# Twenty dots of gathered rows move from VectorE to TensorE and ScalarE; picks and first gathers stand earlier

## The chip, the cores and the metric

The kernel runs on one core of one Trainium2 chip. The metric is the time of one execution on the device in microseconds (us); the kernel before takes 3178.87 us (median of three runs).

## The reference

Two transformer blocks in float32 on 256 tokens of width 2048. Only the end of the second one matters here, a feed-forward of 16384 experts of which each token takes 128:

```python
q = einsum("bsd,dhk->bshk", h, w_pq)                 # queries of 8 heads
sub = einsum("bshpk,hpnk->bshpn", q, peer_keys)      # scores of 2 x 128 keys a head
s, i = top_k(sub, 16)                                # best keys of each side
cand = s[0][:, None] + s[1][None, :]                 # their 256 pairs
top_s, pos = top_k(cand, 16); idx = cidx[pos]        # 16 experts of a head
gate = softmax(top_s)
u = take(peer_u, idx)                                # (128 tokens, 8 x 16, 2048)
a = gelu(einsum("td,thkd->thk", x_blk, u)) * gate    # one dot of 2048 for each
v = take(peer_v, idx)
out = x + einsum("thk,thkd->td", a, v)               # then a norm
```

The tokens are two halves of 128; a half has 8 heads x 16 picks, so there are 2 x 128 = 256 "rows": row n is one expert's row of u for each of the 128 tokens of half n // 128 (one token on each partition), 1 MB.

## The kernel before

Everything up to the key scores is a chain of matmul stages. `out_and_queries_stage` is the last of these: it multiplies w_out and w_peer_q, 8 tiles of 4 slabs, each slab split by ScalarE (L194) and VectorE (L199) into a high and a low part. In its last slabs VectorE already picks the experts of the first four units (a unit is one head of one half): `best_keys`, `best_pairs` and `experts_of_pairs` in turn, which end in `index`, the numbers that a gather needs. Its GpSimd part issues the first 8 gathers once the stage's last matmul is done.

`peer_stage` follows. There:

- GpSimd gathers rows of u (`gather_row`, L1918) into a ring of GR = 8 buffers, `rows`; the gather of row n + 8 waits until row n was read (`freed`), and the first of each 16 also until its unit was picked (`p.picked`).
- VectorE makes one dot for each row (L2308: multiply with h2 and sum, 2048 elements on each partition), in the order of n, into column n of `weight`. Between the dots stand the 36 parts that pick the experts of the other 12 units, spread over the first PICK_DOTS = 232 rows, and a few small steps: `shift` and `share` (the softmax's), `weigh`, `index_pieces`.
- TensorE and ScalarE do nothing until `weigh(0)`, at row 130; then they spread the weights of the first half into `by_expert` (L2384, L2416 to L2432).
- After the last dot VectorE weighs the second half, helps to spread it (L2280, L2285) and adds pieces of v: `add_piece` (L2331) takes gathered half rows of v (L2249). Ahead of the first piece it waits for `summed`, which SyncE loads from x (L2223).
- SyncE loads the first six slabs of v (512 KB each) and then `summed` (1 MB) as soon as the dots 248 to 252 are done; it waits on `freed`.
- TensorE multiplies slabs of v with `by_expert` (L2391) to the end.

The order within an engine is the order in which the program writes it; between engines only semaphores order.

Of the kernel before, what the change touches and what calls it, by code (L numbers as in the profile page):

```python
# [23 lines left out]
ALU = mybir.AluOpType  # L24
AX = mybir.AxisListType

P = 128
# [3 lines left out]
DC = D // P  # L31
# [13 lines left out]
PH, NKEYS, TOPK = 8, 128, 16  # L45
PICKS = PH * TOPK
RING = 4
KPE_W = 256
GR = 8
# [1862 lines left out]
PICK_DOTS = 232  # L1912
# [10 lines left out]
def out_and_queries_stage(core, block, w_out, w_queries, gain_rows, keys_in_dram, x_home, peer_u, p):  # L1923
# [9 lines left out]
    nc, base, outs = core.nc, core.tiles, core.outs  # L1933
# [10 lines left out]
    with ExitStack() as local:  # L1944
# [5 lines left out]
        p.x_kept = x_kept  # L1950
# [147 lines left out]
        @block.gpsimd  # L2098
        def _(pool):
            pool.wait_ge(core.slabs_used, (base + 8) * RING + 2)  # L2100
            pool.wait_ge(p.picked, 1)
            for n in range(GR):
                gather_row(nc, p, n, peer_u)
# [54 lines left out]
def peer_stage(core, block, p, peer_u, peer_v, counts, gain, out):  # L2158
# [14 lines left out]
    nc = core.nc  # L2173
# [4 lines left out]
    with ExitStack() as local:  # L2178
# [3 lines left out]
         pieces_indexed, slab_used) = core.new(  # L2182
# [3 lines left out]
            "stored", "final_steps", "pieces_used", "pieces_indexed", "expert_slabs_used")  # L2186
# [4 lines left out]
        place = core.place  # L2191
        by_expert = place("by_expert", [P, NH, NKEYS, P], at=-48 * KB)
# [19 lines left out]
        def half_of(half):  # L2212
            return slice(half * PICKS, (half + 1) * PICKS)

# [22 lines left out]
        @block.gpsimd  # L2237
        def _(pool):
            for n in range(GR, UNITS * TOPK):
                if n % TOPK == 0:  # L2240
                    pool.wait_ge(p.picked, n // TOPK + 1)
                pool.wait_ge(freed, n + 1)
                gather_row(nc, p, n, peer_u)
            pool.wait_ge(freed, NH * PICKS + GR)
            pool.wait_ge(pieces_indexed, NH)
            for n in range(UNITS * TOPK):
                if n >= GR:
                    pool.wait_ge(piece_used, n - GR + 1)
                nc.gpsimd.indirect_dma_start(  # L2249
                    pieces[:, n % GR, :], None, v_pieces,  # L2250
                    bass.IndirectOffsetOnAxis(ap=piece_at[n % NH][:, n // NH:n // NH + 1], axis=0)
                ).then_inc(piece_landed[n % GR], 16)

        @block.vector
        def _(dve):
# [45 lines left out]
            parts_left = 3 * (UNITS - EARLY_UNITS)  # L2301
            for u in range(UNITS):
                for j in range(TOPK):
                    n = u * TOPK + j
                    dve.wait_ge(landed[n % GR], n // GR * 16 + 16)
                    if n:
                        dve.wait_ge(freed, n + GR - 1)
                    nc.vector.tensor_tensor_reduce(out=junk[:, n % 2, :], in0=rows[:, n % GR, :], in1=p.h2[:, u // PH, :],  # L2308
                                                   scale=1.0, scalar=0.0, op0=ALU.mult, op1=ALU.add,
                                                   accum_out=weight[:, n:n + 1]).then_inc(freed, 1)  # L2310
                    k = n * parts_left // PICK_DOTS
                    if k < (n + 1) * parts_left // PICK_DOTS and k < parts_left:
                        PICK_PARTS[k % 3](core, dve, step, EARLY_UNITS + k // 3, p.sub, p)
                    if n in (4 * TOPK + 6, PICK_DOTS + 1):
                        shift(u // PH)
                    if n in (5 * TOPK + 6, 15 * TOPK + 6):
                        share(u // PH)
                    if j == 2 and u == PH:
                        weigh(0)
                    if n == PICK_DOTS + 4:  # L2320
                        index_pieces()
# [43 lines left out]
        def _(pe):  # L2365
# [29 lines left out]

            turn(0)
# [12 lines left out]
        def _(act):  # L2409
# [43 lines left out]
            exponentiate(0)  # L2453
# [218 lines left out]
```

## Time and profile before

| | |
|---|---|
| median of three runs | 3178.87 us (3177.93 to 3179.3) |
| the profiled execution's own time | 3179.94 us |
| its span, first to last instruction | 3177.8 us |
| VectorE busy over the span | 2180.5 us (69%) |
| TensorE busy | 2404.4 us (76%) |
| ScalarE busy | 1109.8 us (35%) |
| row 0's dot starts | 1942.45 us |
| row 150's dot starts | 2347.15 us |
| row 255's dot starts, the last | 2619.75 us |
| the first piece of v is added | 2631.05 us |
| TensorE and ScalarE spread the first half's weights | 2301 to 2466 us |

The span's times count from the first instruction. Busy shares are means over stages that have different limits; the stretch of the dots, from 1942 to 2622 us, has to be read by itself.

### The profile page before, as it was taken

Reading aid. Unit: us, or ns where it says so; the run is one execution under the profiler, and the core shown is the slowest. Engines: PE = TensorE matmul, PEld = TensorE weight load, DVE = VectorE, ACT = ScalarE, POOL = GpSimd, SP = SyncE. Lnnn points to the kernel's source line nnn. Section 1 sums busy time; section 2 is a strip of 40 time slices with the busy share of each in tenths; the row PEclk is TensorE's granted clock in tenths of the full one; section 3 lists DMA queues with packets and bytes.
Section 4 is the critical chain, followed back from the end, with each engine's and each line's share of the span. In section 5 each row is a group of like instructions: output and inputs, shape, how many; then the busy total and the mean of one; then the engine's idle time right before and its main releaser. Section 6 shows DMA issues by size and latency. Waiting matters only on the chain. (4 is left out here: it accounts for less than half of the span.)

```text
span 3177.8 us, 29960 instructions
## 1 busy us (share of the span) xinstructions
PE 2404.4 (76%) x10393; PEld 1830.5 (58%) x10393; DVE 2180.5 (69%) x2958; ACT 1109.8 (35%) x1876; POOL 826.6 (26%) x571
## 2 busy tenths in 40 slices
PE   6899999999999999999999993000033006999993
PEld 5667778888888878888777893000033005444441
DVE  3997565544454565555546568999999998565668
ACT  4345554344434444535554441000099005000000
POOL 0300001010100000000000004767667664544445
PEclk9999999999999999999999997555555559999997
DMA  8443455665656546546435666999999995999998
GB/s 224 150 148 113 167 173 189 195 186 194 189 185 186 197 159 218 185 147 205 140 113 167 210 205 253 419 389 387 392 396 389 396 398 188 405 410 409 409 409 342
DMA packets 294486, 813.25 MB, mean 256 GB/s; under 512 B 33113, under 2 KB 73281, under 8 KB 260320
## 3 DMA queue, kind: packets, MB, share of 16 engines
q1 hardware_dynamic: 220400, 408.87, 38.8%
q0 software_dynamic: 73728, 402.69, 31.9%
q8 instruction: 67, 1.10, 0.1%
q14 instruction: 51, 0.42, 0.0%
q10 hardware_dynamic: 240, 0.18, 0.0%
HBM read 807.48 MB, written 4.19 MB: 255 GB/s over the span
## 5 line engine op out<-in xcount | busy, mean ns | idle before, releaser
L199 DVE TENSOR_TENSOR wl<-ring,wh 128x1024 fp32r<-128x1024 f32 (+2 forms) x616 | 732.7, 1231 | 646.0 <-ACT wh L194 643.4
L194 ACT CAST wh<-ring 128x1024 fp32r<-128x1024 f32 (+2 forms) x616 | 609.4, 1039 | 672.7 <-PE ps L215 620.5
L213 PE MATMUL ps<-wh,th 128*128 128x512 f32 (+1 forms) x1632 | 646.3, 396 | 27.8 <-DVE wl L199 23.0
L1918 POOL DMA_INDIRECT expert_rows<-in_peer_u,index x256 | 481.9, 1882 | 626.8 <-PE ps L2004 437.9
L214 PE MATMUL ps<-wl,th 128*128 128x512 f32 (+1 forms) x1632 | 637.2, 390 | 0.0
L215 PE MATMUL ps<-wh,tl 128*128 128x512 f32 (+1 forms) x1632 | 636.9, 390 | 0.0
L2308 DVE CUSTOM_DVE_ANT_0 junk<-expert_rows,h 128x2048 f32<-128x2048 f32 x256 | 570.1, 2286 | 6.2 <-DMA expert_rows<-in_peer_u,index 5.3
L2331 DVE SCALAR_TENSOR_TENSOR x_and_pieces<-expert_pieces,const,x_and_pieces 128x1024 f32<-128x1024 f32 x256 | 327.7, 1283 | 170.5 <-DMA expert_pieces<-in_peer_v,piece_index 83.4
L2391 PE MATMUL ps<-expert_slabs,by_expert 128*128 128x512 f32 x1024 | 439.7, 592 | 0.7 <-ACT by_expert L2432 0.7
L213 PEld LDWEIGHTS ps<-wh,th 128*128 128x128 f32 x1632 | 309.8, 190 | 98.9 <-issue 18.7
L215 PEld LDWEIGHTS ps<-wh,tl 128*128 128x128 f32 x1632 | 309.6, 190 | 64.7
L214 PEld LDWEIGHTS ps<-wl,th 128*128 128x128 f32 x1632 | 310.1, 190 | 61.1
L2391 PEld LDWEIGHTS ps<-expert_slabs,by_expert 128*128 128x128 f32 x1024 | 194.5, 190 | 245.3 <-issue 244.4
L2373 PE MATMUL ps<-const,keys_of 128*128 128x128 f32 x4 | 1.4, 448 | 316.2 <-DVE index L1903 316.2
L803 POOL TENSOR_TENSOR square<-relu 128x512 f32<-128x512 f32 x32 | 48.4, 1536 | 661.3 <-ACT relu L758 661.3
L2384 PE MATMUL ps<-col_hot,row_hot 128*128 128x128 f32 x512 | 105.9, 374 | 128.7 <-ACT row_hot L2427 102.0
L213 PE MATMUL ps<-wh,fh 128*128 128x512 f32 x512 | 199.5, 390 | 0.0
L215 PE MATMUL ps<-wh,fl 128*128 128x512 f32 x512 | 199.2, 389 | 0.0
L214 PE MATMUL ps<-wl,fh 128*128 128x512 f32 x512 | 199.2, 389 | 0.0
L2373 PEld LDWEIGHTS ps<-const,keys_of 128*128 128x128 f32 x4 | 0.6, 204 | 316.7 <-DVE index L1903 316.7
L2384 PEld LDWEIGHTS ps<-col_hot,row_hot 128*128 128x128 f32 x512 | 92.2, 267 | 142.5 <-ACT col_hot L2421 57.8
L2249 POOL DMA_INDIRECT expert_pieces<-in_peer_v,piece_index x128 | 133.5, 1043 | 138.3 <-DVE x_and_pieces L2331 124.4
(329 smaller groups left out, 2668.9 us busy)
## 6 DMA issues: line engine op xcount, KB each, us to landing
ring<-in_w_in SPq DMA_DIRECT2D x80, 1024.0 KB, 5.2
ring<-in_w_up SPq DMA_DIRECT2D x64, 1024.0 KB, 5.5
ring<-in_w_down SPq DMA_DIRECT2D x64, 1024.0 KB, 5.1
expert_slabs<-in_peer_v SPq DMA_DIRECT2D x128, 512.0 KB, 6.8
ring<-in_w_in SPq DMA_DIRECT2D x68, 512.0 KB, 4.8
ring<-in_w_out SPq DMA_DIRECT2D x32, 1024.0 KB, 5.0
ring<-in_w_peer_q SPq DMA_DIRECT2D x16, 1024.0 KB, 5.2
ring<-in_w_ukv SPq DMA_DIRECT2D x8, 1024.0 KB, 5.5
```

The lines of the kernel that those rows point to most:

```text
L194: self.nc.scalar.copy(self.wh[:, i % 2, two, 0:w], self.ring[:, i, two, 0:w]).then_inc(self.high_ready, 1)
L199: self.nc.vector.tensor_tensor(self.wl[:, i % 2, two, 0:w], self.ring[:, i, two, 0:w], self.wh[:, i % 2, two, 0:w].bitcast(F32), ALU.subtr ...
L213: mm(o, hi, wh, start=start and k == 0, stop=False)
L214: mm(o, hi, wl, start=False, stop=False)
L215: last = mm(o, lo, wh, start=False, stop=stop and k == 3)
L803: nc.gpsimd.tensor_tensor(square[:, n % 2, half, :], r, r, ALU.mult).then_inc(squared, 1)
L1918: nc.gpsimd.indirect_dma_start(p.rows[:, n % GR, :], None, peer_u, bass.IndirectOffsetOnAxis(ap=p.index[:, n:n + 1], axis=0)).then_inc(p.l ...
L2249: nc.gpsimd.indirect_dma_start(pieces[:, n % GR, :], None, v_pieces, bass.IndirectOffsetOnAxis(ap=piece_at[n % NH][:, n // NH:n // NH + 1] ...
L2308: nc.vector.tensor_tensor_reduce(out=junk[:, n % 2, :], in0=rows[:, n % GR, :], in1=p.h2[:, u // PH, :], scale=1.0, scalar=0.0, op0=ALU.mu ...
L2331: nc.vector.scalar_tensor_tensor(out=summed[:, half, :], in0=pieces[:, n % GR, :], scalar=weight[:, c:c + 1], in1=summed[:, half, :], op0= ...
L2384: mm(core.ps[:, 4 + i // 4, i % 4 * P:(i % 4 + 1) * P], row_hot[:, i, :], col_hot[:, i, :], start=True, stop=True).then_inc(hot_used, 1)
L2391: end = mm(core.ps[:, 2 * half + q, :], by_expert[:, half, m, :], slabs[:, m % SLOTS, q * 512:(q + 1) * 512], start=m == 0, stop=m == NKEY ...
```

## The change

Twenty of the rows of the first half, n = 4, 10, ..., 118, are no longer read by VectorE. TensorE turns the row's 16 blocks of 128 x 128 (`turn_row`, into PSUM banks 0 to 3), ScalarE copies each bank to SBUF (`lay_row`, four copies of 512), and TensorE multiplies the 16 blocks with the 16 blocks of h2, turned once at the start in the same way, into one 128 x 128 product, whose diagonal holds the 128 dots. VectorE reads that diagonal seven rows later (`diagonal`: multiply with the identity and sum, 128 elements). A buffer that held such a row is free for the next gather when TensorE has turned it. The pick parts are spread over the first 150 rows in place of 232; `shift(1)` and `index_pieces` keep their places. The first eight gathers no longer wait for the stage's last matmul but each for the last reader of what its buffer lies on. ScalarE's `exponentiate(0)` follows its copies of row 70, and TensorE's `turn(0)` follows row 118.

```diff
-PICK_DOTS = 232
+PICK_DOTS = 150
+LATE_DOT = 232
+PE_ROWS = tuple(range(4, 120, 6))
+PE_LAG = 7
...
+        p.x_kept, p.h2_ready = x_kept, h2_ready
...
         @block.gpsimd
         def _(pool):
-            pool.wait_ge(core.slabs_used, (base + 8) * RING + 2)
             pool.wait_ge(p.picked, 1)
             for n in range(GR):
+                if n < RING:
+                    pool.wait_ge(core.low_ready, (base + 7) * (2 * RING) + (2 * n + 2))
+                else:
+                    pool.wait_ge(core.slabs_used, (base + 7) * RING + (RING + 1 + n % 2))
                 gather_row(nc, p, n, peer_u)
...
+        h2_turned = place("h2_turned", [P, DC, P], at=0)
+        row_turned = place("row_turned", [P, DC, P], at=8 * KB)
...
+        by_order = []
+        for n in range(UNITS * TOPK):
+            by_order += [n] * (n not in PE_ROWS) + [n - PE_LAG] * (n - PE_LAG in PE_ROWS)
+
+        def row_read(n):
+            if n in PE_ROWS:
+                return quarters_turned, 4 * (PE_ROWS.index(n) + 2)
+            return freed, GR + by_order.index(n) + 1
...
-                pool.wait_ge(freed, n + 1)
+                pool.wait_ge(*row_read(n - GR))
                 gather_row(nc, p, n, peer_u)
...
+            def dot(n):
+                dve.wait_ge(landed[n % GR], n // GR * 16 + 16)
+                k = by_order.index(n)
+                if k:
+                    dve.wait_ge(freed, k + GR - 1)
+                nc.vector.tensor_tensor_reduce(out=junk[:, k % 2, :], in0=rows[:, n % GR, :], in1=p.h2[:, n // PICKS, :],
+                                               scale=1.0, scalar=0.0, op0=ALU.mult, op1=ALU.add,
+                                               accum_out=weight[:, n:n + 1]).then_inc(freed, 1)
+
+            def diagonal(n):
+                i, k = PE_ROWS.index(n), by_order.index(n)
+                dve.wait_ge(rows_dotted, i + 1)
+                dve.wait_ge(freed, k + GR - 1)
+                nc.vector.tensor_tensor_reduce(out=junk[:, k % 2, 0:P], in0=core.ps[:, (7, 5)[i % 2], 0:P],
+                                               in1=core.ident, scale=1.0, scalar=0.0, op0=ALU.mult, op1=ALU.add,
+                                               accum_out=weight[:, n:n + 1]).then_inc(freed, 1)
+
             for u in range(UNITS):
                 for j in range(TOPK):
                     n = u * TOPK + j
-                    dve.wait_ge(landed[n % GR], n // GR * 16 + 16)
-                    if n:
-                        dve.wait_ge(freed, n + GR - 1)
-                    nc.vector.tensor_tensor_reduce(out=junk[:, n % 2, :], in0=rows[:, n % GR, :], in1=p.h2[:, u // PH, :],
-                                                   scale=1.0, scalar=0.0, op0=ALU.mult, op1=ALU.add,
-                                                   accum_out=weight[:, n:n + 1]).then_inc(freed, 1)
+                    if n not in PE_ROWS:
+                        dot(n)
+                    if n - PE_LAG in PE_ROWS:
+                        diagonal(n - PE_LAG)
                     k = n * parts_left // PICK_DOTS
                     if k < (n + 1) * parts_left // PICK_DOTS and k < parts_left:
                         PICK_PARTS[k % 3](core, dve, step, EARLY_UNITS + k // 3, p.sub, p)
-                    if n in (4 * TOPK + 6, PICK_DOTS + 1):
+                    if n in (4 * TOPK + 6, LATE_DOT + 1):
                         shift(u // PH)
                     if n in (5 * TOPK + 6, 15 * TOPK + 6):
                         share(u // PH)
                     if j == 2 and u == PH:
                         weigh(0)
-                    if n == PICK_DOTS + 4:
+                    if n == LATE_DOT + 4:
...
+            def turn_row(src, banks_read):
+                if banks_read:
+                    pe.wait_ge(quarters_laid, banks_read)
+                for c in range(DC):
+                    last = nc.tensor.transpose(core.ps[:, c // 4, c % 4 * P:(c % 4 + 1) * P], src[:, c * P:(c + 1) * P], core.ident)
+                    if c % 4 == 3:
+                        last.then_inc(quarters_turned, 1)
+
+            def dot_by_tensor(i, n):
+                pe.wait_ge(landed[n % GR], n // GR * 16 + 16)
+                turn_row(rows[:, n % GR, :], 4 * i + 4)
+                if i >= 2:
+                    pe.wait_ge(freed, GR + by_order.index(PE_ROWS[i - 2]) + 1)
+                for c in range(DC):
+                    if c % 4 == 0:
+                        pe.wait_ge(quarters_laid, 4 * (i + 1) + c // 4 + 1)
+                    last = mm(core.ps[:, (7, 5)[i % 2], 0:P], row_turned[:, c, :], h2_turned[:, c, :],
+                              start=c == 0, stop=c == DC - 1)
+                last.then_inc(rows_dotted, 1)
+
+            pe.wait_ge(core.outs_free, (core.outs - 1) * 2 + 6)
+            pe.wait_ge(p.scores_out, 2 * 4)
+            pe.wait_ge(p.h2_ready, 1)
+            turn_row(p.h2[:, 0, :], 0)
+            for i, n in enumerate(PE_ROWS):
+                dot_by_tensor(i, n)
             turn(0)
...
-            exponentiate(0)
+            def lay_row(dst, i):
+                for q in range(4):
+                    act.wait_ge(quarters_turned, 4 * i + q + 1)
+                    if i >= 2 and q == 0:
+                        act.wait_ge(rows_dotted, i - 1)
+                    nc.scalar.copy(dst[:, 4 * q:4 * q + 4, :], core.ps[:, q, :].rearrange("p (c t) -> p c t", c=4)).then_inc(
+                        quarters_laid, 1)
+
+            lay_row(h2_turned, 0)
+            for i, n in enumerate(PE_ROWS):
+                lay_row(row_turned, i + 1)
+                if n == 4 * TOPK + 6:
+                    exponentiate(0)
```

Three places where the instructions stand otherwise. GpSimd, the first gathers; what stands in brackets is what each waits for (the name after `waits` in the second stage's rows is only that of a semaphore number used before for something else: it is `freed` or, in its one row here, `row_quarters_turned`). Before:

```order
L2098 UNCONDITIONAL_BRANCH [waits barrier_Pool_Activation_PE_DVE_SP_gather]
L1918 DMA expert_rows<-in_peer_u,index 128x2048 [waits unit_picked_16,slabs_used]
L1918 DMA expert_rows<-in_peer_u,index 128x2048 x7
L2237 UNCONDITIONAL_BRANCH
L1918 DMA expert_rows<-in_peer_u,index 128x2048 [waits taps_in_1] x8
```

And now:

```order
L1921 DMA expert_rows<-in_peer_u,index 128x2048 [waits low_ready,unit_picked_16]
L1921 DMA expert_rows<-in_peer_u,index 128x2048 [waits low_ready] x3
L1921 DMA expert_rows<-in_peer_u,index 128x2048 [waits slabs_used] x4
L2255 UNCONDITIONAL_BRANCH
L1921 DMA expert_rows<-in_peer_u,index 128x2048 [waits taps_in_1] x4
L1921 DMA expert_rows<-in_peer_u,index 128x2048 [waits normed_4]
L1921 DMA expert_rows<-in_peer_u,index 128x2048 [waits taps_in_1] x3
```

The eight first gathers have waits of their own, and gather 12 waits for row 4's turning. VectorE, the dots ahead of the third pick part (`experts_of_pairs`, L1895); `ISA junk` is a dot (or, from `ps`, a diagonal), and each is followed by a short `ISA const` that stores its sum. Before:

```order
L2308 ISA junk,const<-expert_rows,h_12674 128x2048
L2308 ISA const 128x1
L2308 ISA junk,const<-expert_rows,h_12674 128x2048
L2308 ISA const 128x1
L1895 TENSOR_TENSOR one_hot<-const,place_f 128x256 x2
```

And now:

```order
L2326 ISA junk,const<-expert_rows,h_12674 128x2048
L2326 ISA const 128x1
L2334 ISA junk,const<-ps,const 128x128
L2334 ISA const 128x1
L2326 ISA junk,const<-expert_rows,h_12674 128x2048
L2326 ISA const 128x1
L2326 ISA junk,const<-expert_rows,h_12674 128x2048
L2326 ISA const 128x1
L1895 TENSOR_TENSOR one_hot<-const,place_f 128x256 x2
```

A diagonal has come in, and a pick part follows every fourth or fifth row in place of every sixth or seventh. TensorE, between the key scores and `turn(0)`. Before:

```order
L2016 MATMUL ps<-keys_turned,peer_queries_turned 128x128 x8
L2364 UNCONDITIONAL_BRANCH
L2373 MATMUL ps<-const,keys_of 128x128 x2
L2376 MATMUL ps<-const 128x128
L2397 UNCONDITIONAL_BRANCH
```

And now, with 19 more pairs like the last two ahead of the transposes of `keys_of`:

```order
L2019 MATMUL ps<-keys_turned,peer_queries_turned 128x128 x8
L2398 UNCONDITIONAL_BRANCH
L2434 MATMUL ps<-const,h_12674 128x128 x16
L2434 MATMUL ps<-const,expert_rows 128x128 x16
L2446 MATMUL ps<-h_turned,row_turned 128x128 x16
```

TensorE's queue now holds 16 transposes and 16 matmuls for each of the 20 rows, in front of everything else that it does in this stage.

## Rows read from the trace of the kernel before

**Rows 1.** Windows: PE, PEld, DVE, ACT, POOL busy us, TensorE's clock, DMA share, GB/s.

```profile
2030.00:2050.00 20.00, 0.00 (x0) 0.00 (x0) 19.66 (x35) 0.00 (x0) 14.13 (x8) 0.50 1.01 420
...
2250.00:2270.00 20.00, 0.00 (x0) 0.00 (x0) 19.86 (x23) 0.00 (x0) 14.96 (x9) 0.50 0.97 378
...
2310.00:2330.00 20.00, 8.29 (x32) 7.12 (x32) 19.86 (x33) 19.71 (x58) 11.75 (x7) 0.50 0.99 395
...
2590.00:2610.00 20.00, 0.00 (x0) 0.00 (x0) 19.90 (x22) 0.00 (x0) 15.22 (x8) 0.50 1.01 419
```

**Rows 2.** Waits of VectorE and of GpSimd, 1900 to 2600 (us, times, longest).

```profile
DVE junk L2308 <- DMA expert_rows<-in_peer_u,index: 5.3, 7, 2.5
...
POOL expert_rows L1918 <- DVE const L2308: 120.8, 36, 4.1
```

**Rows 3.** Timeline of ScalarE, GpSimd and VectorE where the dots begin (start, us, engine).

```profile
1938.73 1.52 ACT L2073 ACTIVATE key_scores<-ps,small 128x512 f32<-128x512 f32 x2 [1.31 <-PE ps L2016]
...
1926.04 2.36 DVE L199 TENSOR_TENSOR wl<-ring,wh 128x1024 fp32r<-128x1024 f32 x2 [2.35 <-ACT wh L194]
...
1936.61 1.15 POOL L1918 DMA_INDIRECT expert_rows<-in_peer_u,index  x1 [437.93 <-PE ps L2004]
...
1942.45 2.29 DVE L2308 CUSTOM_DVE_ANT_0 junk<-expert_rows,h 128x2048 f32<-128x2048 f32 x1 [2.54 <-DMA expert_rows<-in_peer_u,index]
```

**Rows 4.** Timeline of VectorE, dots on either side of the three pick parts.

```profile
2060.76 2.29 DVE L2308 CUSTOM_DVE_ANT_0 junk<-expert_rows,h 128x2048 f32<-128x2048 f32 x1
...
2062.97 2.29 DVE L2308 CUSTOM_DVE_ANT_0 junk<-expert_rows,h 128x2048 f32<-128x2048 f32 x1
...
2068.37 2.29 DVE L2308 CUSTOM_DVE_ANT_0 junk<-expert_rows,h 128x2048 f32<-128x2048 f32 x1
...
2079.44 2.28 DVE L2308 CUSTOM_DVE_ANT_0 junk<-expert_rows,h 128x2048 f32<-128x2048 f32 x1
...
2084.60 2.29 DVE L2308 CUSTOM_DVE_ANT_0 junk<-expert_rows,h 128x2048 f32<-128x2048 f32 x1
...
2563.97 0.76 DVE L1895 TENSOR_TENSOR one_hot<-const,place_f 128x256 f32<-128x256 f32 x2
...
2566.66 2.29 DVE L2308 CUSTOM_DVE_ANT_0 junk<-expert_rows,h 128x2048 f32<-128x2048 f32 x1
```

**Rows 5.** Timeline of VectorE: the dots of rows 150, 247 and 255, and small operations.

```profile
2347.15 2.29 DVE L2308 CUSTOM_DVE_ANT_0 junk<-expert_rows,h 128x2048 f32<-128x2048 f32 x1
...
2602.04 2.29 DVE L2308 CUSTOM_DVE_ANT_0 junk<-expert_rows,h 128x2048 f32<-128x2048 f32 x1
...
2619.75 2.28 DVE L2308 CUSTOM_DVE_ANT_0 junk<-expert_rows,h 128x2048 f32<-128x2048 f32 x1
2621.96 0.08 DVE L2308 DVE_READ_ACCUMULATOR2_ANT const<- 128x1 f32 x1
...
2625.27 1.10 DVE L2280 TENSOR_SCALAR row_hot<-const,turned_keys,turned_weight 128x128 f32<-128x128 f32 x4
2631.05 1.28 DVE L2331 SCALAR_TENSOR_TENSOR x_and_pieces<-expert_pieces,const,x_and_pieces 128x1024 f32<-128x1024 f32 x1 [4.68 <-DMA x_and_pieces<-out]
```

**Rows 6.** TensorE: 16 transposes, four matmuls (8 records), lengths of all such records.

```profile
1854.20 1.91 PE L1991 MATMUL ps<-const,keys 128*128 128x128 f32 x16
...
2316.62 2.08 PE L2384 MATMUL ps<-col_hot,row_hot 128*128 128x128 f32 x8 [3.09 <-ACT row_hot L2427]
...
L2384 PE MATMUL ps<-col_hot,row_hot x512: 275/421/583, 2301.5 to 2689.3; 128*128 128x128 f32 x171
```

**Rows 7.** L1918 from 2070 to 2560: from issue to landing.

```profile
DMA to landing us min/median/max: 7.1/9.4/11.3
```

**Rows 8.** Row 255's gather in GpSimd's timeline, and L1918 from 2585 to 2606.

```profile
2605.45 1.91 POOL L1918 DMA_INDIRECT expert_rows<-in_peer_u,index  x1 [0.30 <-issue]
...
DMA to landing us min/median/max: 9.3/10.5/14.2
```

**Rows 9.** The first pieces of v (L2249) from 2600 to 2640: from issue to landing.

```profile
DMA to landing us min/median/max: 5.9/8.3/8.6
```

More of the change, by code:

```diff
@@ L1949, in out_and_queries_stage @@
             "factor_steps", "keys_turned", "keys_copied", "scored", "scores_out", "h2_ready", "pick_steps")
-        p.x_kept = x_kept
+        p.x_kept, p.h2_ready = x_kept, h2_ready
         p.picked, = core.new("unit_picked")
@@ L2181, in peer_stage @@
          iota_in, sums_in, x_back, gain_in, added, sums, mean_ready, rooted, normed, stored, final, piece_used,
-         pieces_indexed, slab_used) = core.new(
+         pieces_indexed, slab_used, quarters_turned, quarters_laid, rows_dotted) = core.new(
             "dve_done", "rows_used", "shifted", "exponentiated", "gelued", "weighted", "picks_turned",
@@ L2185, in peer_stage @@
             "sums_in", "x_back", "gain_in", "x_added", "x_sums", "mean_ready", "rooted", "normed",
-            "stored", "final_steps", "pieces_used", "pieces_indexed", "expert_slabs_used")
+            "stored", "final_steps", "pieces_used", "pieces_indexed", "expert_slabs_used",
+            "row_quarters_turned", "row_quarters_laid", "rows_dotted")
         cols_hot = core.new("cols_hot_low", "cols_hot_high")
```

## The prediction

> **What bounds the kernel now.** I read the windows first. Through the dots VectorE is busy 19.7 to 19.9 us of every 20, and TensorE does nothing or little [rows 1]. But the DMA share is 0.97 to 1.01 as well, so that view alone names two candidates. The bytes part them: about 420 GB/s while the ring of eight buffers fills (2030), 378 in the middle (2250), and 419 again near the end (2590), where VectorE has no picks left [rows 1]. In the middle the DMA moves less than it can. The waits say why: VectorE waited for a gathered row 5.3 us in all, in seven waits, the longest of them on row 0; GpSimd waited 120.8 us for VectorE to read a buffer [rows 2]. So the dots and the picks, one after the other on VectorE, bound this stretch. The DMA is the limit close behind: 1.049 MB at 420 GB/s is 2.50 us a row. A dot takes 2.21 us (2060.76 to 2062.97), and the three pick parts of a unit add 5.40 - 2.21 = 3.19, 5.16 - 2.21 = 2.95 and 2.69, together 8.83 us [rows 4]. Spread over 232 rows the 12 units (106 us) add 0.46 to each row: 2.67 us, above 2.50. That is the order of things which the change disturbs: a row without picks costs VectorE 2.21, less than the DMA's 2.50.
>
> **The start.** VectorE's first dot waits 2.54 us for row 0, whose gather was issued at 1936.61, after the stage's last matmul [rows 3]. Now gathers 0 to 3 follow VectorE's last four splits (the last ends at 1928.4 [rows 3]); one takes under 6 us to land here (1936.61 to 1942.45), so those rows are there when VectorE is ready. It then waits for ScalarE's scores, which end at 1938.73 + 1.52 = 1940.25 [rows 3]. First dot at 1940.3, 2.1 us earlier. The small waits on rows 1 to 6 go too.
>
> **The first 150 rows.** VectorE has 130 dots there x 2.213 = 287.7 us and all 36 pick parts = 106.0. `shift`, `share` and `weigh` stand in this stretch as before, about 1.5. The 20 diagonals are not in this trace. Below, four operations on 128 elements take 1.10 [rows 5], with the 0.08 of the accumulator's read 0.36 or less each; a dot of 2048 takes 2.21, of which at most 2.13 scales with its length by the same 0.08. I take 0.30 each, between 0.20 and 0.50: 6.0 us. Row 150 would be reached at 1940.3 + 287.7 + 106.0 + 1.5 + 6.0 = 2341.5, where it was at 2347.15 [rows 5]. This is the trap in the arithmetic: twenty dots less save 20 x (2.21 - 0.30) = 38 us, but 82 rows' worth of picks (about 37 us) come in from behind, so that the stretch itself gains next to nothing. What the change wins must come out of the 106 rows behind it.
>
> **Those 106 rows.** VectorE could do them in 2.21 us each, the DMA in 2.50. So the DMA becomes the bound once the stock of landed rows is used up. How large is the stock? Before, the gather for row 255 was issued at 2605.45, 3.4 us after dot 247 started at 2602.04 [rows 5, 8]; one takes 9.4 us to land [rows 7]; the dot of the row then stands eight rows of 2.67 later: 21.4 - 3.4 - 9.4 = 8.6 us of lead. With the picks denser it is a little more; I take 9, bounds 8 to 12. Row 150 landed at 2332.5, row 255 lands 105 x 2.50 = 262.5 later, at 2595.0.
>
> **The crowd at the end.** SyncE releases six slabs (3 MB) and `summed` (1 MB) with dots 248 to 252. Before, the last rows had a lead; still the slowest of the last gathers took 14.2 us in place of 9.4 to 10.5 [rows 8]. Now VectorE has no lead, six rows are still to come at that point, and the other 4 MB get in among them: at least nothing, at most 4 x 2.50 = 10 us. I take 6.5, above the 4.8 measured with fewer rows outstanding. Row 255 at 2601.5, its dot done at 2603.8. The Trainium skill (DMA: Bandwidth & Descriptors, section Queues, rings and completion order) says that each DMA engine serves its queues in turn, a packet at a time; by equal turns the 3 MB of slabs would all pass beside the last rows, 7.5 us, and the sum would be 1 us longer than mine. The slow gather agrees with it in kind.
>
> **The pieces.** The stage behind hangs on VectorE, so its start moves with the last dot. But its first wait, 4.68 us, is not wholly a gift: `add_piece(0)` started at 2631.05, 9.0 us after the last dot's end at 2622.04 [rows 5]; the row names `summed`, yet the first piece, issued only after the last dot, needs 5.9 to 8.6 us to land [rows 9]. `summed` will be early now, the piece won't: 0.3 + 7. The first piece is added at 2603.8 + 7.3 = 2611.1, and everything behind it keeps its distance. Gain: 2631.05 - 2611.1 = 20 us. Against the profiled execution's 3179.94 that is 3160, against the median of the runs, which is 1.1 lower, **3159**.
>
> **What hides TensorE's and ScalarE's part.** 16 transposes took 1.91 us at the full clock; the clock stood at 0.50 (1.2 GHz) all through the dots even with TensorE busy 8.3 of 20 us [rows 1, 6], so I count 3.8. Four matmuls of 128 x 128 (two records each) took 2.08 at that clock [rows 6]: 16 take 8.3. The turning overlaps three of ScalarE's four copies (a 512-wide read of PSUM took 0.76 [rows 3]); the last may stand in the open. About 12.5 us a row. VectorE needs five dots, a diagonal and 1.44 pick parts for six rows, 11.1 + 0.3 + 4.2 = 15.6 us, and asks for the diagonal seven rows later. Cover: 3 us a row. A buffer is free after the turning, 4 us after landing, sooner than its dot would have freed it. Queued behind all this are `turn(0)` on TensorE, `exponentiate(0)` and `gelu(0)` on ScalarE; the latter are wanted at rows 86 and 130, long after rows 70 and 118, and the spreading of the first half, which went from 2301 to 2466 (the table above), ends long before 2604 too. The Trainium skill (TensorE: Matmul & The Clock Gate, section Part 4: PE-mode transpose) says that transposes don't count as work for the clock; that speaks for the low level, by which I counted. No row here shows this mixture; were the clock full, the chain would be near 6 us and the sum the same.
>
> **The rivals.**
> - *TensorE's chain is too long: slower.* If a row took TensorE more than 15.6 us, each of the 20 diagonals would hold up VectorE. The gain is eaten at 15.6 + 20/20 = 16.6, and beyond 16.9 the kernel is measurably slower. For it: single records last 0.42 us in the median [rows 6]; without overlap, 48 of them and four copies are 23 us, 20 x 7.6 = 150 us late: 3310. Against: groups of eight took 2.08, not 3.4. 6 in 100.
> - *The DMA can't do better in this stretch than the middle shows: no change.* At 390 GB/s a row takes 2.69, 105 rows 20 us more than I count: 3179. For it: a DMA share of 0.97 at 378 GB/s. Against: 419 at 2590 with the same kind of gather, and VectorE never waiting. 7 in 100.
> - *The ceiling is above 420: faster than I say.* With VectorE the bound to the end, the 38 us and the 2 of the start would be had whole: 3138, at 474 GB/s, which no window shows. 5 in 100 for anything below 3149. Of this kind is the figure of 436 GB/s in the Trainium skill (DMA: Bandwidth & Descriptors, section Bandwidth): by it a row takes 2.40 and the kernel 3149; the windows stop at 420.
> - *Some TensorE rows or gathers come late without deciding it,* 3169 to 3178: 5 in 100.
>
> **How the numbers follow.** My forecast has 77 in 100. Its own range comes from the bounds: a crowd of nothing, a lead of 12 and a diagonal of 0.20 would give some 11 us less, but `summed` and the piece still have to land, so 3149; a crowd of 10, a piece of 8.6, a lead of 8 and diagonals of 0.50 give 10 more, 3169. That range is mine for 8 in 10 too, a microsecond wider on either side. Runs of this kernel lie within 0.05% of one another, and 0.2%, 6.4 us, is about what can be told from no change. Faster: 77, the high ceiling 5 and half of the last rival, 85; within: most of the second rival and the rest of the last, 9; slower: 6.
>
> **What the profile will show.** If I am right: the first dot near 1940.3 with no wait; row 150 near 2341; from about 30 rows later small waits of VectorE on `expert_rows`, 0.2 to 0.3 us each, some 15 to 25 us in all, with about 420 GB/s; GpSimd waiting less for VectorE; the dots at the end 3 us apart or more; the last one done near 2604. Waits of the diagonals on TensorE (`ps`) would show the first rival, 390 GB/s with VectorE waiting the second, no waits on rows the third. Wrong I would be most easily in the crowd at the end, in the lead, or if TensorE's rows hold the ring back.

## The result and the profile after

The changed kernel takes 3157.82 us (median of four runs, 3157.04 to 3158.88) against 3179.09 in the same comparison: 0.993 of the time, 95% interval 0.9916 to 0.9945, 21.3 us faster. Predicted were 3159 us and a range of 3148 to 3170. The profiled execution took 3158.3 us, its span is 3156.5.

Windows of 20 us of the changed kernel; after the time stand the busy us of PE, PEld, DVE, ACT and POOL, then TensorE's granted clock, the DMA share and GB/s (the counterpart of [rows 1]).

```profile
2040.00:2060.00 20.00, 10.09 (x63) 9.71 (x61) 19.66 (x44) 2.34 (x4) 14.78 (x9) 0.74 1.01 408
...
2160.00:2180.00 20.00, 12.97 (x80) 12.78 (x79) 19.62 (x43) 4.69 (x8) 14.72 (x8) 0.72 1.01 417
...
2300.00:2320.00 20.00, 7.37 (x29) 6.35 (x29) 19.73 (x38) 19.61 (x58) 11.94 (x8) 0.50 0.98 379
2320.00:2340.00 20.00, 7.36 (x31) 6.20 (x29) 19.66 (x35) 19.61 (x59) 13.88 (x8) 0.50 0.88 352
2340.00:2360.00 20.00, 8.22 (x32) 7.04 (x32) 20.00 (x19) 19.61 (x59) 15.86 (x8) 0.50 0.95 369
2360.00:2380.00 20.00, 8.28 (x32) 7.12 (x32) 20.00 (x19) 19.71 (x59) 17.26 (x10) 0.50 1.01 421
...
2460.00:2480.00 20.00, 0.00 (x0) 0.00 (x0) 18.45 (x17) 0.00 (x0) 17.56 (x9) 0.50 1.01 419
...
2580.00:2600.00 20.00, 0.00 (x0) 0.00 (x0) 12.17 (x12) 0.00 (x0) 0.00 (x0) 0.50 1.01 402
```

Three stretches are to be seen. From 1960 to 2360 VectorE is full, and the DMA is so only in some windows: it moves 370 to 419 GB/s up to 2320, then 352 and 369 in the two windows around row 150 (2339.44), where the picks end. From 2360 to 2580 the DMA is at its 420, and from 2410 on VectorE idles some 1.5 us of 20. At 2580 VectorE is down to 12 of 20 while the DMA still moves 402 GB/s. The waits (us, times, longest) from 1900 to 2620, answering to [rows 2]:

```profile
DVE junk L2326 <- DMA expert_rows<-in_peer_u,index: 20.6, 65, 2.0
...
POOL expert_rows L1921 <- DVE const L2326: 76.0, 27, 3.6
...
POOL expert_rows L1921 <- DVE const L2334: 19.6, 9, 2.9
```

VectorE now waits for rows 65 times, where it waited seven times. GpSimd waits 95.6 us for VectorE, dots and diagonals together, where it waited 120.8. The timeline of VectorE (start, us) at the places of [rows 3, 5], the dots of rows 0, 150, 182, 183, 254 and 255, and the first piece:

```profile
1938.75 2.29 DVE L2326 CUSTOM_DVE_ANT_0 junk<-expert_rows,h 128x2048 f32<-128x2048 f32 x1 [0.28 <-ACT key_scores L2076]
...
2339.44 2.29 DVE L2326 CUSTOM_DVE_ANT_0 junk<-expert_rows,h 128x2048 f32<-128x2048 f32 x1
...
2410.49 2.29 DVE L2326 CUSTOM_DVE_ANT_0 junk<-expert_rows,h 128x2048 f32<-128x2048 f32 x1 [0.16 <-DMA expert_rows<-in_peer_u,index]
2412.98 2.29 DVE L2326 CUSTOM_DVE_ANT_0 junk<-expert_rows,h 128x2048 f32<-128x2048 f32 x1 [0.19 <-DMA expert_rows<-in_peer_u,index]
...
2596.30 2.29 DVE L2326 CUSTOM_DVE_ANT_0 junk<-expert_rows,h 128x2048 f32<-128x2048 f32 x1 [1.50 <-DMA expert_rows<-in_peer_u,index]
2600.60 2.29 DVE L2326 CUSTOM_DVE_ANT_0 junk<-expert_rows,h 128x2048 f32<-128x2048 f32 x1 [2.00 <-DMA expert_rows<-in_peer_u,index]
...
2607.59 1.29 DVE L2365 SCALAR_TENSOR_TENSOR x_and_pieces<-expert_pieces,const,x_and_pieces 128x1024 f32<-128x1024 f32 x1 [0.35 <-DMA expert_pieces<-in_peer_v,const]
```

No dot waits for a row up to row 181; from 182 on they stand 2.49 us apart, and the last 4.3. No diagonal waits for TensorE. One diagonal, and one row's work on TensorE and ScalarE with the idle time ahead (timelines of the three engines):

```profile
1967.03 0.28 DVE L2334 CUSTOM_DVE_ANT_0 junk<-ps,const 128x128 f32<-128x128 f32 x1
...
2190.05 3.67 PE L2434 MATMUL ps<-const,expert_rows 128*128 128x128 f32 x16 [8.41 <-DMA expert_rows<-in_peer_u,index]
2193.51 4.53 PE L2446 MATMUL ps<-h_turned,row_turned 128*128 128x128 f32 x32
...
2192.90 0.59 ACT L2518 COPY row_turned<-ps 128x512 f32<-128x512 f32 x1 [0.27 <-PE ps L2434]
```

TensorE needs 8 us for a row and then waits 7 to 9.5 us for the next.

### The profile page after: what moved, and what is told of

It reads as the page before. It is cut to its first block and busy times, and to the rows that moved or that the text cites. A ratio compares the mean times of both kernels' runs of the same rounds, so it can differ in the third digit from the quotient of the medians.

```text
span 3156.5 us, 32054 instructions
## 1 busy us (share of the span) xinstructions
PE 2554.3 (81%) x11369; PEld 1977.6 (63%) x11369; DVE 2146.8 (68%) x2958; ACT 1157.2 (37%) x1960; POOL 830.9 (26%) x571
## 5 line engine op out<-in xcount | busy, mean ns | idle before, releaser
L2326 DVE CUSTOM_DVE_ANT_0 junk<-expert_rows,h 128x2048 f32<-128x2048 f32 x236 | 532.1, 2290 | 21.9 <-DMA expert_rows<-in_peer_u,index 20.6
L2434 PE MATMUL ps<-const,expert_rows 128*128 128x128 f32 x320 | 70.6, 412 | 154.8 <-DMA expert_rows<-in_peer_u,index 153.9
L2267 POOL DMA_INDIRECT expert_pieces<-in_peer_v,const x128 | 131.4, 1027 | 152.1 <-DVE x_and_pieces L2365 118.5
```

The costliest lines, as they stand in the source:

```text
L2267: nc.gpsimd.indirect_dma_start(pieces[:, n % GR, :], None, v_pieces, bass.IndirectOffsetOnAxis(ap=piece_at[n % NH][:, n // NH:n // NH + 1] ...
L2326: nc.vector.tensor_tensor_reduce(out=junk[:, k % 2, :], in0=rows[:, n % GR, :], in1=p.h2[:, n // PICKS, :], scale=1.0, scalar=0.0, op0=ALU ...
L2434: last = nc.tensor.transpose(core.ps[:, c // 4, c % 4 * P:(c % 4 + 1) * P], src[:, c * P:(c + 1) * P], core.ident)
```

## The experiments

Each kernel was timed beside the kernel before on the same chip. The first four take the change apart, the next three load one suspected place each, the last three follow what the first four showed. The kernel before came out at 3178.77 to 3180.26 us in the four sets of runs, so a difference of 1 or 2 us between kernels of different sets says nothing. Where a time of landing is given, it is a gather's issue plus its time from issue to landing.

**The picks alone.** In the kernel before; `shift(1)` and `index_pieces` stay at row 232.

```diff
-PICK_DOTS = 232
+PICK_DOTS = 150
+LATE_DOT = 232
```

> Of the change only the picks: all 36 parts in the first 150 rows, every dot on VectorE, gathers as before. My theory (VectorE and the DMA bound the dots in turn, VectorE at 2.21 us a row plus picks, the DMA at 2.50): rows 0 to 149 now cost VectorE 2.92 us each, so row 150's dot starts near 1942.5 + 4 + 332 + 106 + 2 = 2386; the last 106 rows go at 2.50 with 10 us of lead used up, the last dot ends near 2647: slower by some 20 us, 3200. Rival (each part of the change gives something of its own, and denser picks cost nothing, since VectorE's work is the same): 3179, no change.

Measured: 3202.39 us, 1.0073 of before (1.0056 to 1.009). Two windows of 40 us, one in the picks and one behind them:

```profile
2300.00:2340.00 40.00, 4.62 (x17) 3.75 (x17) 39.52 (x67) 11.51 (x35) 24.88 (x14) 0.50 0.95 359
2500.00:2540.00 40.00, 0.00 (x0) 0.00 (x0) 35.92 (x33) 0.00 (x0) 33.37 (x16) 0.50 1.01 420
```

Row 150 starts at 2384.34 (forecast 2386). While the picks last, the DMA moves about 360 GB/s and loses time that VectorE then cannot win back, because the rows behind come at 420. The same work in another order costs 23 us.

**TensorE's rows alone.** In the changed kernel; the first gathers wait as before.

```diff
-PICK_DOTS = 150
+PICK_DOTS = 232
...
+            pool.wait_ge(core.slabs_used, (base + 8) * RING + 2)
             pool.wait_ge(p.picked, 1)
             for n in range(GR):
-                if n < RING:
-                    pool.wait_ge(core.low_ready, (base + 7) * (2 * RING) + (2 * n + 2))
-                else:
-                    pool.wait_ge(core.slabs_used, (base + 7) * RING + (RING + 1 + n % 2))
                 gather_row(nc, p, n, peer_u)
```

> Of the change only the twenty rows on TensorE and ScalarE: picks over 232 rows as before, first gathers as before. My theory: rows 0 to 125 cost VectorE some 2.35 us each, less than the DMA's 2.50, so they go at 2.50 and row 125 stands 26 us earlier; from there VectorE is the bound again at 2.67, builds a lead up, and there is no crowd at the end. The last dot ends near 2596, against 2622 before: 3153, so the whole change would not beat its first part. Rival (the picks' move is needed to cash the twenty dots in): the gain stays under 10 us, 3170 or more.

Measured: 3161.22 us, 0.9948 (0.9932 to 0.9965), 17.8 us faster where I had said 26. A window of 40 us, and VectorE's waits from 1900 to 2620:

```profile
2120.00:2160.00 40.00, 21.88 (x142) 21.30 (x141) 35.73 (x67) 8.53 (x14) 26.38 (x16) 0.76 1.01 420
...
DVE junk L2323 <- DMA expert_rows<-in_peer_u,index: 21.4, 40, 2.7
```

The direction of my reading holds: the part alone does nearly what the whole change does, and the rival's "under 10" falls. The DMA moves 419 to 421 GB/s in every window from 1940 to 2300, so it bounds these rows, as I said. The size was off: row 126 starts at 2263.18, 18.9 us earlier than before, not 26. Row 8 landed 21.3 us behind row 0 and not 20 (1942.2 to 1963.5), the next 118 rows came 2.52 us apart and not 2.50 (row 126 landed at 2260.9), and row 126's dot starts 2.3 us later still, because VectorE was busy. Together these are about 6 of the 7 us.

**The early gathers alone.** In the kernel before.

```diff
-            pool.wait_ge(core.slabs_used, (base + 8) * RING + 2)
             pool.wait_ge(p.picked, 1)
             for n in range(GR):
+                if n < RING:
+                    pool.wait_ge(core.low_ready, (base + 7) * (2 * RING) + (2 * n + 2))
+                else:
+                    pool.wait_ge(core.slabs_used, (base + 7) * RING + (RING + 1 + n % 2))
                 gather_row(nc, p, n, peer_u)
```

> Of the change only the first eight gathers. My theory: the first dot starts when the scores are ready, 2 us earlier, the six small waits on rows 1 to 6 (2.8 us) go, and VectorE stays the bound to the end: 5 us less, 3174. Rival (gathers in the queries stage get in the way of its slabs or of VectorE's splits, or the picks catch up): no change, 3179.

Measured: 3174.41 us, 0.9985 (0.9975 to 0.9994): 4.6 us faster, as expected. One wait of 0.28 us is all that is left on the dots.

**The change without the picks' move.** In the changed kernel.

```diff
-PICK_DOTS = 150
+PICK_DOTS = 232
```

> The change without the picks' move: twenty rows on TensorE, early gathers, picks over 232 rows. My theory: the first 125 rows are bound by the DMA, and here the early gathers count whole: row 8 lands near 1948 and row 125 near 2240, 14 us before its time with late gathers; then VectorE at 2.67 a row. Last dot near 2582, first piece near 2591: 3139, some 19 us faster than the whole change. Rival (the parts add up to the whole change's 3158, and the move of the picks has a part in that gain): 3158 or slower.

Measured: 3148.43 us, 0.9909 (0.9892 to 0.9925): 9.4 us faster than the whole change. The windows, one among TensorE's rows and one behind them:

```profile
2100.00:2120.00 20.00, 8.16 (x48) 7.97 (x48) 19.16 (x31) 3.94 (x6) 15.75 (x9) 0.73 1.01 419
2260.00:2280.00 20.00, 4.62 (x17) 3.74 (x17) 19.76 (x28) 13.49 (x40) 13.65 (x7) 0.50 1.02 421
```

The DMA moves 418 to 422 GB/s all through from 1960 to 2280, where the changed kernel has stretches at 373. The waits of VectorE from 1900 to 2620:

```profile
DVE junk L2326 <- DMA expert_rows<-in_peer_u,index: 11.5, 24, 2.7
DVE x_and_pieces L2365 <- DMA expert_pieces<-in_peer_v,const: 3.7, 1, 3.7
```

The waits lie between rows 41 and 122; behind them VectorE is the bound, keeps a lead, and no row waits at the end. The early gathers are worth 12.8 us here and 4.6 without TensorE's rows. Where the DMA is the bound, its earlier start counts nearly whole: row 8 landed at 1949.6, 13.9 us earlier than in the kernel with late gathers, and row 126 starts 12.0 us earlier (2251.17 for 2263.18). My 3139 was 9 too low, and all of it lies ahead of row 126: row 125 starts at 2248.74, forecast near 2240. Row 8 landed 1.6 us later than I had said (the DMA moved 389 GB/s between 1940 and 1960), the 118 rows behind it came 2.54 us apart, and row 126's dot stands 2.3 us behind its landing, as above. Why rows cost 2.52 to 2.54 us on average, where most neighbours stand 2.49 apart, stays open.

**TensorE's matmuls made twice, and five times.** In `dot_by_tensor` of the changed kernel; in the second kernel the count is `5 * DC`.

```diff
-                for c in range(DC):
-                    if c % 4 == 0:
+                for t in range(2 * DC):
+                    c = t % DC
+                    if t < DC and c % 4 == 0:
```

> The whole change with the 16 matmuls of each TensorE row made twice (the second result takes the place of the first). In the changed kernel a row took TensorE 3.7 + 4.5 us. My theory (15.6 us a row are covered): 12 to 13 us are covered too: no change from 3158. Rival (TensorE's part is near its limit and holds buffers or diagonals): slower by 5 us or more.

Measured: 3157.44 us, 0.9934 (0.9918 to 0.9951), no change from 3157.82. One row in the timeline of TensorE:

```profile
2194.92 3.67 PE L2434 MATMUL ps<-const,expert_rows 128*128 128x128 f32 x16 [4.58 <-DMA expert_rows<-in_peer_u,index]
2198.39 8.46 PE L2447 MATMUL ps<-h_turned,row_turned 128*128 128x128 f32 x64
```

This row takes TensorE 11.9 us, and TensorE still idled 4.6 us ahead of it.

> The same with the matmuls made five times. My theory: a row takes TensorE some 21 to 23 us, 5 to 7 beyond the 15.6 that VectorE leaves it; VectorE waits for each of the 20 diagonals, the waits add up to some 100 us and come out nearly whole: 3240 to 3280. Rival (buffers and the later rows' slack take it up): under 3180.

Measured: 3225.65 us, 1.0147 (1.013 to 1.0164). A window of 40 us, and the timeline of TensorE, a row and the beginning of the next:

```profile
2160.00:2200.00 40.00, 40.00 (x362) 40.00 (x361) 28.83 (x51) 5.71 (x10) 19.78 (x12) 1.00 0.85 325
...
2181.60 1.91 PE L2434 MATMUL ps<-const,expert_rows 128*128 128x128 f32 x16
2183.35 18.03 PE L2447 MATMUL ps<-h_turned,row_turned 128*128 128x128 f32 x160
2201.22 1.91 PE L2434 MATMUL ps<-const,expert_rows 128*128 128x128 f32 x16
```

And VectorE's waits from 1900 to 2620:

```profile
DVE junk L2334 <- PE ps L2447: 65.3, 18, 5.6
```

A row takes 19.6 us (2181.60 to 2201.22) and 18 diagonals wait 65.3 us in all, which come out as 67.8 us of time. So the mechanism of the prediction's first rival exists, beyond a limit between 12 and 19.6 us, and the changed kernel is far from it with 8. My size (80 to 120 us slower) was too large: I had a row at 21 to 23 us, and it took 19.6, 4 more than the 15.6 that VectorE leaves, with the clock granted at 1.00 all the while; and the first two diagonals did not wait.

**The slabs behind the last dot.** In SyncE's program of the changed kernel.

```diff
-            for m in range(SLOTS):
-                sp.wait_ge(freed, NH * PICKS + m // 2 + 1)
-                sp.dma_start(slabs[:, m], v_rows[:, m, 0:HALF]).then_inc(slab_in[m], 16)
             sp.wait_ge(freed, NH * PICKS + 4)
             sp.wait_ge(p.x_kept, 16)
             sp.dma_start(summed[:], rows_out[:, :, HALF:D]).then_inc(sums_in, 16)
+            for m in range(SLOTS):
+                sp.wait_ge(freed, NH * PICKS + GR)
+                sp.dma_start(slabs[:, m], v_rows[:, m, 0:HALF]).then_inc(slab_in[m], 16)
```

The load of `summed` goes out when dot 251 is done, as in the kernel before (2613.22 there; the slabs follow dots 248 to 250).

> The whole change with the six first slabs of v loaded only after the last dot, and the load of summed alone with dot 252 as before. My theory: the last rows land 2.5 us apart to the end, the last dot is done some 6 us earlier (2597 where it was 2603); but the 3 MB now stand beside the first pieces, so that 3 to 4 of the 6 us are given back there: 3155. Rival (the crowd is the DMA's work in another order, and all of it is given back): 3158. Rival (all 6 us are had): 3152.

Measured: 3159.4 us, 0.9945 (0.9928 to 0.9961), not told apart from the whole change. The dot of row 255 starts at 2596.31, 4.3 us earlier; but

```profile
2608.07 1.28 DVE L2365 SCALAR_TENSOR_TENSOR x_and_pieces<-expert_pieces,const,x_and_pieces 128x1024 f32<-128x1024 f32 x1 [5.13 <-DMA expert_pieces<-in_peer_v,const]
```

the first piece is added at 2608.07 where it was 2607.59: the slabs now stand beside the pieces and all is given back. The rival held, not my 3 us of gain. The runs lie between 3156.6 and 3163.48, too far apart to part 3155 from 3158 by themselves; the two places in the trace do it.

**Picks over 200 rows.** In the changed kernel `PICK_DOTS = 200`.

> The whole change with the picks over the first 200 rows in place of 150. My theory: three stretches, row 126 near 2252 (DMA and VectorE level), row 200 near 2455 (VectorE at 2.74), then the DMA at 2.50 with a lead of 9 us and the crowd of slabs at the end: last dot done near 2594, first piece 2599, 3148: level with 232, since what is saved before row 200 is paid by the DMA behind it. Rival (the fewer rows the picks take, the worse, in proportion): 3152.

Measured: 3148.2 us, 0.9897 (0.9881 to 0.9914), as forecast, level with 232. Row 126 starts at 2252.39, row 200 at 2457.38 (forecast 2252 and 2455).

**Two slopes.** In the changed kernel: 25 of the pick parts are spread over the first 126 rows, the others up to row 232.

```diff
-PICK_DOTS = 150
+PICK_TURN, EARLY_PARTS = 126, 25
...
+            def due(n):
+                if n < PICK_TURN:
+                    return n * EARLY_PARTS // PICK_TURN
+                return EARLY_PARTS + (n - PICK_TURN) * (parts_left - EARLY_PARTS) // (LATE_DOT - PICK_TURN)
...
-                    k = n * parts_left // PICK_DOTS
-                    if k < (n + 1) * parts_left // PICK_DOTS and k < parts_left:
+                    k = due(n)
+                    if k < due(n + 1) and k < parts_left:
```

> The kernel with the picks over 232 rows, but in two slopes: 25 of the 36 parts in the first 126 rows, where VectorE stood idle 12 us for the DMA, and 11 in the next 106. My theory: row 126 stays near 2251, rows 126 to 232 cost VectorE 2.53 us each instead of 2.69, about the DMA's 2.50; the last dot ends near 2578, 13 us before that of the uniform spread: 3136. Rival (the waits on rows in the first half are not free time, the added parts push the dots there): 3145 or more.

Measured: 3140.28 us, 0.987 (0.9854 to 0.9887): 17.5 us faster than the whole change, 40 faster than the kernel before, and 8 faster than the even spread over 232 rows (3148.43). Windows of 40 us:

```profile
2200.00:2240.00 40.00, 23.55 (x146) 22.94 (x146) 39.45 (x75) 8.69 (x14) 29.30 (x17) 0.75 1.01 420
2300.00:2340.00 40.00, 15.67 (x61) 13.63 (x62) 39.72 (x58) 39.23 (x115) 29.49 (x16) 0.50 1.01 420
2400.00:2440.00 40.00, 14.52 (x56) 12.47 (x56) 39.73 (x51) 35.53 (x100) 28.51 (x16) 0.50 1.01 414
2500.00:2540.00 40.00, 0.69 (x2) 0.29 (x2) 39.79 (x47) 3.86 (x9) 30.53 (x16) 0.50 1.01 414
```

VectorE's waits for rows:

```profile
DVE junk L2331 <- DMA expert_rows<-in_peer_u,index: 8.5, 5, 2.3
```

Both are full at once: VectorE 39.5 of 40 us, the DMA 414 to 420 GB/s. The five waits are on rows 251 to 255, the rows that share the DMA with the slabs (the prediction's crowd at the end), which I had left out of the 3136.

**24 rows on TensorE.** As two slopes, with

```diff
-PE_ROWS = tuple(range(4, 120, 6))
+PE_ROWS = tuple(range(4, 124, 5))
-PICK_TURN, EARLY_PARTS = 126, 25
+PICK_TURN, EARLY_PARTS = 126, 27
```

and `exponentiate(0)` after row 69.

> As two_slopes, with 24 rows on TensorE (n = 4, 9, ..., 119) and 27 of the parts in the first 126 rows. My theory: VectorE's own work falls by 8 us more, but the DMA needs 2.50 us for each row from 1951 on, 2575 for the last, so the DMA is the bound throughout, without lead, and the crowd of slabs comes back: 3135 to 3141, no better than 20 rows. Rival (VectorE is still the bound): 3129.

Measured: 3138.82 us, 0.9869 (0.9853 to 0.9886), not told apart from 20 rows. VectorE's waits for rows, and the DMA in the middle of TensorE's rows:

```profile
DVE junk L2331 <- DMA expert_rows<-in_peer_u,index: 14.0, 24, 3.0
...
2100.00:2200.00 100.00, 59.44 (x369) 58.10 (x369) 97.69 (x185) 20.25 (x34) 69.35 (x40) 0.76 1.01 419
```

Part of the work taken off VectorE comes back as waits: the DMA is the bound.

## Why the prediction was right

**What bounds it.** VectorE before, the DMA close behind: shown. The picks-only kernel loses 23 us by holding the DMA at about 360 GB/s through the first 150 rows, and in two slopes both are full.

**The start.** First dot forecast at 1940.3, measured 1938.75. In that trace the last split of the stage ahead starts at 1924.50 where it was 1926.04 [rows 3], so 1.5 of the 3.7 us are not the change's. The start of this stage scatters by more than that from kernel to kernel: in the other kernels with early gathers the first dot starts between 1938.4 and 1943.3 (1940.27 in early gathers alone). Early gathers alone gave 4.6 us, the 2.1 and the small waits.

**The first 150 rows.** Forecast 401.2 us from the first dot to row 150 (1940.3 to 2341.5), measured 400.7 (1938.75 to 2339.44). A diagonal is 0.28 us long, taken at 0.30. The forecast that this stretch by itself gains next to nothing held.

**The 106 rows.** The lead is the time from a row's landing to the start of its dot. Forecast: 9 us at row 150, between 8 and 12, and from there 2.50 us a row. The gather of row 150, and its time to landing:

```profile
2318.65 2.74 POOL L1921 DMA_INDIRECT expert_rows<-in_peer_u,index  x1 [3.64 <-DVE const L2326]
...
DMA to landing us min/median/max: 7.2/7.2/7.2
```

Row 150 landed at 2325.9 and its dot started at 2339.44: a lead of 13.6, outside my bounds. But the rows behind it did not come at 2.50 at once. Their gathers wait for buffers that VectorE frees between its last picks, the DMA moves 352 and 369 GB/s up to 2360, and row 182, where VectorE meets the DMA, landed at 2410.5, 2.64 us a row. From row 182 on 2.49 between neighbours is the rule. So two errors of the sum stand against each other here: up to row 249 the forecast was 2580.0 and its dot started at 2578.37. That they nearly cancel is luck.

**The crowd.** Forecast 6.5 us over six rows at 2.50, 21.5 us from row 249 to row 255; measured 22.2 (2578.37 to 2600.60), so a crowd of 7.2. That it is the DMA's work in another order, and the removal of the slabs worth nothing, I had not said; slabs_late showed it.

**The pieces.** Forecast 7.3 us from the last dot's end to the first piece, measured 4.7 (2602.9 to 2607.59): the term was mis-sized. The first piece was issued at 2603.17 and landed 4.3 us later, not 7. I took the latency from a trace in which the slabs were still under way when the pieces were issued (the last landed at 2627.0, the first piece went out at 2622.31); here the last slab had landed at 2602.5, and only `summed` was under way. That this is what made the piece faster agrees with slabs_late, where the slabs went out with the pieces and the first piece was waited for until 2608.07.

**Behind the first piece** I let everything keep its distance. The first piece is 23.5 us earlier (2631.05 to 2607.59), the span 21.3 us shorter, so 2.2 us went in the rest. From the first piece to the end the ten other kernels took 546.9 to 547.7 us, the kernel before 546.7, this trace 548.9. I cannot say what the 1 to 2 us are; it was not tried.

**The sum.** The first piece came 3.5 us earlier than the 2611.1 of the forecast, and 2.2 us were lost behind it: 21.3 us of gain for 20. That the total is right to about 1 us is luck in part; single terms were off by up to 5 us.

**TensorE and ScalarE.** Hidden, as forecast, with more room than I gave them: 8 us a row, not 12.5. The transposes took 3.67 us, near the 3.8 counted for the low clock; the matmuls took 3.7 to 5.0 in place of 8.3, because the clock rose among them (0.67 to 0.76 on average in these windows, between the levels 0.50 and 1.00). In mm_five, with the clock at 1.00 throughout, the same transposes took 1.91 and sixteen matmuls 3.6 (a fifth of 18.03). The Trainium skill's rule that transposes don't count as work for the clock (TensorE: Matmul & The Clock Gate, section Part 4: PE-mode transpose) fits the slow transposes but is not shown by them: TensorE had done nothing for 8 us ahead of them, and the clock stood at 0.50 through idle stretches before the change too [rows 1].

**What I missed.** I read the move of the picks as what lets the DMA-bound rows come into being, and took it for part of the gain. The sum was right and that reading was not: of the three parts, TensorE's rows give 17.8 us, the early gathers 12.8 on top of them, and the picks' move takes 9.4 away. I had the rule for it in the text (picks added to a stretch where VectorE is already the bound cost their full length there) and did not ask what the change would be without them. The 436 GB/s of the Trainium skill (DMA: Bandwidth & Descriptors, section Bandwidth) did not show: where the DMA was the bound, these gathers moved 418 to 422 GB/s before the change and after it, and no 20 us of any run lie above 424.

## What to carry to other kernels

Where two resources are both over 95% busy, the order of the work decides as much as its amount: work that loads one of them has to lie where the other is the bound, and each stretch wants its own rate. Compute the time per item of each resource for each stretch, before and after, and take a compound change apart on paper into its parts; a part may lower the gain. A transfer that looks like a delay at the end of a stretch is only worth moving if the DMA is idle somewhere between that place and the place where its data is needed; here it was not.

## What the runs showed of the hardware

The clock of TensorE was not the same within this one stage: 0.50 with nothing, or with 8 us of one-hot matmuls in 20 (2300 to 2440); 0.67 to 0.76 on average over the windows of TensorE's rows, 8 us of transposes and matmuls in 16; 1.00 throughout with the matmuls made five times, where the same 16 transposes took 1.91 us in place of 3.67.

GpSimd's issue of a gather takes some 0.94 us while VectorE makes picks, and here 1.90 to 2.75 us while it makes dots. GpSimd's timeline in the changed kernel:

```profile
1941.32 2.75 POOL L1921 DMA_INDIRECT expert_rows<-in_peer_u,index  x1 [2.85 <-DVE const L2326]
1944.37 1.91 POOL L1921 DMA_INDIRECT expert_rows<-in_peer_u,index  x1 [0.30 <-issue]
1946.58 1.90 POOL L1921 DMA_INDIRECT expert_rows<-in_peer_u,index  x1 [0.30 <-issue]
1948.79 0.93 POOL L1921 DMA_INDIRECT expert_rows<-in_peer_u,index  x1 [0.30 <-issue]
```

The first ends at 1944.07, the next at 1946.28 and 1948.48: 2.2 us apart, one for each dot, about 0.9 us after a dot has given way to the next (dots started at 1938.75 and 1940.96, and every 2.21 us). That looks as if the last 0.9 us of a gather's issue could begin only when a dot has ended. The whole trace agrees: of its 256 gathers, 192 began while a dot ran, and the shortest of these took 1.28 us; the other 64 took 0.93 to 1.22; and none ended more than 0.91 us into a dot. The kernel before shows the same (213 gathers, the shortest 1.27 us; none ended more than 0.89 us into a dot). It is read from the rows, and no run changed the dots' length to test it. As long as a dot is shorter than the DMA's 2.49 us it costs nothing here: the DMA moved 419 to 422 GB/s from 2360 to 2580 with issues of 1.9 us and more. By this reading a longer VectorE instruction of the same kind would hold the gathers up. The Trainium skill (SBUF — State Buffer, section SBUF: two separate sides) describes VectorE's two-port modes keeping GpSimd from writing the descriptors of its DMAs; the trace agrees in kind, though whether these dots, with two SBUF inputs, run in such a mode no run here shows.
